# Two transformer blocks on one core: norm of the state-space branch two steps deep, rotary embedding moved to VectorE, and three edits of the order of weight splits and modulation products

## What is computed

```python
for l in range(2):      # first block: mod = silu(c) @ ada_w[l] + ada_b[l], nine vectors of 1024
    h = h + 0.5 * (1 + mod[2]) * swiglu(modulate(rmsnorm(h), mod[0], mod[1]), wg, wu, wd)
    proj = modulate(rmsnorm(h), mod[3], mod[4]) @ w_in
    y_ret = retention(rq, rk, rv, rg)       # rope(q), rope(k), decayed scores, rmsnorm, * silu(g)
    y_sb = stick_breaking(sq, sk, sv)
    y_ssm = mamba2(z, xbc, dt, ...)         # ends in rmsnorm(y * silu(z), norm_gain)
    h = h + (1 + mod[5]) * (concat(y_ret, y_sb, y_ssm) @ w_out)
    h = h + 0.5 * (1 + mod[8]) * swiglu(modulate(rmsnorm(h), mod[6], mod[7]), ...)

def rope(x):            # x1, x2: the lower and upper half of a head's 128 dimensions
    return concat([x1 * cos - x2 * sin, x1 * sin + x2 * cos])
```

## Time and profile before

| what | value |
|---|---|
| median of three runs | 1975.79 us (1975.63 to 1977.26) |
| the profiled execution | 1976.52 us, span 1974.4 us |
| TensorE busy | 1924.0 us (97%) |
| VectorE busy | 1499.2 us (76%) |
| ScalarE busy | 1065.5 us (54%) |
| GpSimd busy | 175.8 us (9%) |
| one split by ScalarE (L1334), by VectorE (L1914), one product (L1889) | mean 1045, 1234 and 1250 ns |
| granted TensorE clock | 0.997 of full speed, mean |

### The profile page before, as it was taken

One profiled execution on the slowest core, in us unless ns is written; L12 is line 12 of the kernel. 1 busy time (PEld: TensorE's weight loads), 2 busy tenths in 40 slices (PEclk: granted clock), 3 DMA queues, 4 the chain that ended last, 5 costly groups with the idle time before them and its releaser, 6 DMA issues.

```text
span 1974.4 us, 38148 instructions
## 1 busy us (share of the span) xinstructions
PE 1924.0 (97%) x15902; PEld 1881.0 (95%) x15902; DVE 1499.2 (76%) x2287; ACT 1065.5 (54%) x1712; POOL 175.8 (9%) x182
## 2 busy tenths in 40 slices
PE   7999999999999999999999999999999999999998
PEld 6999999899999999999899999999999999999998
DVE  7767787887787777878877787878777777788553
ACT  5644655474546544654664455465644455557453
POOL 0000012120011000022211000000210000002000
PEclk9999999999999999999999999999999999999999
DMA  9778575557785777666567865566587765555552
GB/s 379 281 258 320 185 261 203 203 207 259 268 318 212 264 276 262 217 226 224 208 248 281 300 224 197 192 206 234 199 284 275 269 223 195 200 208 189 194 193 107
DMA packets 83837, 466.40 MB, mean 236 GB/s; under 512 B 9424, under 2 KB 9552, under 8 KB 44496
## 3 DMA queue, kind: packets, MB, share of 16 engines
q1 hardware_dynamic: 48544, 334.98, 47.0%
q10 hardware_dynamic: 35120, 128.99, 18.4%
HBM read 462.88 MB, written 1.05 MB: 235 GB/s over the span
## 4 chain that ended last, share of the span: by engine, by line
PE 56%; DVE 9%; ACT 5%; issue 1%; POOL 0%; DVEq 0%; ACTq 0%
PE bank L737 55%; DVE low L1914 3%; ACT high L1334 2%; DVE ada_ring L1889 1%; PE bank L1135 1%; DVE u_split L1963 1%; DVE v L1956 0%; ACT full L1473 0%; DVE h L2060 0%; DVE region L2421 0%; ACT sil L1481 0%; DVE rope_t L2101 0%; ACT L1481 0%; DVE sil L2106 0%; ACT v L1355 0%
## 5 line engine op out<-in xcount | busy, mean ns | idle before, releaser
L1914 DVE TENSOR_TENSOR low<-ring,high 128x1024 fp32r<-128x1024 f32 x616 | 751.6, 1234 | 295.7 <-issue 179.5
L737 PE MATMUL bank<-u_split,high 128*128 128x256 f32 x5664 | 741.2, 280 | 9.2 <-DVE u_split L1963 5.1
L737 PEld LDWEIGHTS bank<-u_split,high 128*128 128x128 f32 x5664 | 691.9, 188 | 17.5 <-DVE u_split L1963 7.6
L1334 ACT ACTIVATE high<-ring 128x1024 fp32r<-128x1024 f32 x616 | 618.0, 1045 | 77.7 <-PE bank L737 51.2
L737 PE MATMUL bank<-u_split,low 128*128 128x256 f32 (+1 forms) x2832 | 410.2, 278 | 0.0
L737 PEld LDWEIGHTS bank<-u_split,low 128*128 128x128 f32 (+1 forms) x2832 | 362.9, 188 | 0.4
L1889 DVE SCALAR_TENSOR_TENSOR ada_ring<-ada_ring,cond 128x1024 f32<-128x1024 f32 x242 | 302.5, 1250 | 0.0
L737 PE MATMUL bank<-hid,high 128*128 128x256 f32 x2112 | 269.2, 277 | 0.0
L737 PEld LDWEIGHTS bank<-hid,high 128*128 128x128 f32 x2112 | 253.8, 188 | 0.0
L1533 ACT ACTIVATE sil<-bank 128x256 f32<-128x256 f32 x107 | 41.2, 385 | 199.5 <-PE bank L737 199.4
L737 PE MATMUL bank<-hid,low 128*128 128x256 f32 x1056 | 148.1, 277 | 0.0
(11 more groups left out here) (240 smaller groups left out, 2073.7 us busy)
## 6 DMA issues: line engine op xcount, KB each, us to landing
ring<-stream SPq DMA_DIRECT2D x302, 1024.0 KB, 5.8
ada_ring<-ada ACTq DMA_DIRECT2D x240, 512.0 KB, 4.5
region<-ada SPq DMA_DIRECT2D x6, 1024.0 KB, 12.9
ring<-stream SPq DMA_DIRECT2D x4, 640.0 KB, 4.8
region<-na_bias ACTq DMA_DIRECT2D x2, 1024.0 KB, 5.2
ring<-stream SPq DMA_DIRECT2D x4, 512.0 KB, 4.5
cst<-const SPq DMA_DIRECT2D x1, 1600.0 KB, 8.3
cond<-cond SPq DMA_DIRECT2D x2, 512.0 KB, 6.5
```

What stands on the lines that cost most here:

```text
L737: return pe.e.matmul(out, lhs, rhs, start=start, stop=stop, skip_group_check=True)
L1334: act.e.activation(hi, src, ACT.Copy).then_inc(*act.done(("high", n)))
L1914: dve.e.tensor_tensor(lo, src, hi.bitcast(F32), ALU.subtract).then_inc(*dve.done(("low", n)))
```

## The change

It has five parts.

1. Rotary embedding without TensorE and GpSimd: VectorE multiplies the bank by cos into SBUF, multiplies the two halves of the partitions by sin into a second tile, each half read from the other half's partitions and one with factor -1, and adds. This is done in the turn in which q and k are finished; the piece ret_rope, its matmul and its bank are gone.
2. The norm of the state-space branch scales tile j before it subtracts for tile j-1.
3. The four grains of the retention gate (sg) take no modulation products (rate 0 instead of 0.75).
4. wanted_first asks for one grain more in each of the turns 3 to 8, instead of one in each second turn.
5. In the down part of every feed-forward the additions (and ScalarE's squares) stand ahead of the turn's split and products.

```diff
-        side[18 + h].append((0, "ret_rope", h))
...
-    if key[0] in ("xbc", "dt", "sz"):
+    if key[0] in ("xbc", "dt", "sz", "sg"):
         return 0.0
-    if key[0] in ("sv", "sq", "sk", "sg", "rv", "rq", "rk"):
+    if key[0] in ("sv", "sq", "sk", "rv", "rq", "rk"):
         return RATE_HEADS
...
-    return 18 if t < 3 else 19 if t < 5 else 20 if t < 7 else 21
+    return 18 + max(0, t - 2)
...
         for n in range(FT):
-            split(first + 2 * FT + n + 1 + AHEAD)
-            ada(dve.ada.turns(rate_of(("down", f, n))))
             for d in range(KT - 1):
                 if SUMMED[d] == n - 1:
                     add(d)
+            split(first + 2 * FT + n + 1 + AHEAD)
+            ada(dve.ada.turns(rate_of(("down", f, n))))
         add(KT - 1)
...
-                    for j in range(4):
-                        y = m.sy[:, j, :]
-                        dve.e.scalar_tensor_tensor(out=y, in0=y, scalar=m.pa(l, "sgn", j, 1), in1=r, op0=ALU.mult,
-                                                   op1=ALU.mult).then_inc(*dve.done(("ssm_scaled", l, j)))
-                        dve.wait_ge(("y_high", l, 8 + j))
-                        rest(m.y_sb, 4 + j, y, ("y", l, 8 + j))
+                    for j in range(5):
+                        if j < 4:
+                            y = m.sy[:, j, :]
+                            dve.e.scalar_tensor_tensor(out=y, in0=y, scalar=m.pa(l, "sgn", j, 1), in1=r, op0=ALU.mult,
+                                                       op1=ALU.mult).then_inc(*dve.done(("ssm_scaled", l, j)))
+                        if j:
+                            dve.wait_ge(("y_high", l, 7 + j))
+                            rest(m.y_sb, 3 + j, m.sy[:, j - 1, :], ("y", l, 7 + j))
...
             dve.wait_ge(("full", "rqk", l, h))
-            copy(m.rqk[:, h, :], m.banks[dve.bank("rqk", l, h)], ("out", "rqk", l, h), ("rqk", l, h))
+            dve.e.tensor_tensor(two(m.rqk[:, h, :]), two(b), spread(cos, 2), ALU.mult).then_inc(*dve.done(("ret_cos", l, h)))
+            if h:
+                dve.wait_ge(("roped", l, h - 1))
+            dve.e.scalar_tensor_tensor(out=two(t2[up]), in0=two(b[down]), scalar=-1.0, in1=spread(sin[down], 2), op0=ALU.mult,
+                                       op1=ALU.mult).then_inc(*dve.done(("ret_sin", l, h)))
+            dve.e.tensor_tensor(two(t2[down]), two(b[up]), spread(sin[up], 2), ALU.mult) \
+                .then_inc(*dve.done(("out", "rqk", l, h), ("ret_sin", l, h)))
+            dve.wait_ge(("ret_cos", l, h), ("ret_sin", l, h))
+            dve.e.tensor_tensor(m.rqk[:, h, :], m.rqk[:, h, :], t2, ALU.add).then_inc(*dve.done(("roped", l, h)))
```

More of the change, by code:

```diff
@@ L1056, in side @@
                     values(b, m.sv, i, m.tb[3 * (i % 2) + 1]).then_inc(*pe.done(("sb_values", l, i)))
-                elif piece == "ret_rope":
-                    b = banks.take("work", "ret_rope", l, i)
-                    pe.wait_ge(("rqk", l, i))
-                    mm(b[:, 0:2 * T], m.c1("rot"), m.rqk[:, i, :], True, True).then_inc(*pe.done(("ret_rot", l, i)))
                 elif piece == "ret_scores":
@@ L2261, in side @@
                     rest(m.y_sb, i, b[:, 0:T], ("out", "sb_values", l, i), ("y", l, 4 + i))
-                elif piece == "ret_rope":
-                    b = m.banks[dve.bank("ret_rope", l, i)]
-                    t1, t2 = m.rope_t[:, 0:512], m.rope_t[:, 512:1024]
-                    dve.wait_ge(("ret_rot", l, i))
-                    if i:
-                        dve.wait_ge(("roped", l, i - 1))
-                    dve.e.tensor_tensor(two(t2), two(b[:, 0:512]), spread(m.c1("sin"), 2), ALU.mult) \
-                        .then_inc(*dve.done(("out", "ret_rope", l, i), ("ret_sin", l, i)))
-                    dve.wait_ge(("ret_cos", l, i), ("ret_sin", l, i))
-                    dve.e.tensor_tensor(m.rqk[:, i, :], t1, t2, ALU.add).then_inc(*dve.done(("roped", l, i)))
                 elif piece == "ret_scores":
@@ L2577, in side @@
                     pool.e.tensor_tensor(w, w, m.c1("before"), ALU.mult).then_inc(*pool.done(("sb_weight", l, i)))
-                elif piece == "ret_rope":
-                    pool.wait_ge(("rqk", l, i))
-                    if i:
-                        pool.wait_ge(("roped", l, i - 1))
-                    pool.e.tensor_tensor(two(m.rope_t[:, 0:512]), two(m.rqk[:, i, :]), spread(m.c1("cos"), 2), ALU.mult) \
-                        .then_inc(*pool.done(("ret_cos", l, i)))
                 elif piece == "ret_norm":
```

4 lines of the change are left out of this document (3 added, 1 removed).

## The result

The changed kernel takes 1984.56 us (median of 4 runs, 1984.06 to 1986.92), the kernel before 1975.71 beside it: ratio 1.0047, 95% interval 1.003 to 1.0063. It is slower by more than the 0.2% that can be told. That is 8.8 us more by the medians. The forecast was 1979.1, 3.3 us more, with a range of 1971.5 to 1985.5.

A forecast was written before the change was run, and what follows sets the result against it. TensorE, fed during 1924.0 of 1974.4 us, was taken as the bound. Terms -6.6 (rope, norm), +8.0 and +2.2 (sg products), 0.0 (splits), -0.3 (additions) summed to +3.3: 1979.1 us, range 1971.5 to 1985.5.

The forecast's parts named there:

- Rope and norm, -6.6: Both layers' mixers: parts 1 and 2 together save 3.3 us a layer, between 1.5 and 5.
- a new wait eats most of the two rotations, and 0.5 is left: Ahead of the state-space norm: TensorE gains 1.6 us, then waits 1.1 for ScalarE's last square.
- The retention wait: TensorE's wait for the first retention head's square, 1.20 us before; TensorE was to go on 1.6 us earlier.
- the slow product of 2.04 at 344.09: First mixer: a modulation product slowed from 1.21 us beside GpSimd's product; removing that gives back 0.8 to 1.1 a head.
- The burst, +8.0: Second feed-forward, behind the third addition: five products instead of one, with stands for loads, cost 8.0 us (4.6 to 10).
- Ahead of the second block, +2.2: Two missing products of 1.14 us delay the gain columns and TensorE's first matmul there by 2.2 us (1.8 to 2.5).
- First feed-forward, 0.0: Part 4: the 1.54 us wait at 79.68 goes but returns as about 1.5 near 86.3; between -1.6 and +0.6.
- Additions first, -0.3: Part 5: stages end with a less late last addition; -0.3 us over four feed-forwards, between -1 and +1.
- (b): First feed-forward: without the wait, TensorE's quick pace saves 4.6 us plus 1.5 of wait, giving 1973.0; chance 0.1.
- Rival (a): Second feed-forward: loads land in time, the five products cost 2 us instead of 8, giving 1973.1; chance 0.15.
- (d): Second feed-forward's five products cost little and the rope pays in full: 10 us below forecast, 1969; chance 0.05.
- Rival (c): Mixers: VectorE's extra rope work holds TensorE longer, a layer keeps 1 us, -2 instead of -6.6, 1983.7; chance 0.2.

The follow-up runs named there:

- sg undone: The changed kernel with the retention gate's four grains taking modulation products again (0.75 each); 1977.19 us, ratio 0.9999.
- the other pair: Kernel before with deeper norm, earlier splits and additions ahead of splits (ratio 0.998), against the same without the additions moved (1970.85 us, 0.9972).
- two experiments: Changed kernel with rate 0.46 in the second feed-forward's gate and up part, 1.0031; kernel before with deeper norm and products moved out of its down part, 0.9991.
- additions first alone: The kernel before with only the additions and squares put ahead of the splits and products in the down parts; ratio 1.0005.
- rope behind side: Changed kernel with the retention gate's products restored and VectorE's four rope instructions per head behind the turn's mixer pieces; 1973.91 us, ratio 0.9994.
- later products: Kernel before, deeper norm, rate 0.45 in the second feed-forward's down part, 0.46 in gate and up parts of second and third; 1974.46 us, ratio 0.9991.
- the first four: First experiments: changed kernel with part 3 undone (1977.19 us); kernel before with part 3 (1990.01), part 1 (1978.05) or part 2 (1972.58) only.

## Why the prediction came out as it did

The sign and the place of the loss were right, the size was not: 3.3 forecast, 8.8 measured, near the upper end of the range. By its own steps, with the slow excess taken out:

**Rope and norm, -6.6.** Measured -2.6 and -3.2, in sum -5.8. The sum was nearly right by luck, for its make-up was wrong. I gave the matmuls that go most of it, and the norm the rest; alone, the rope is worth -1.1 and the norm about -4 (-5.3 in its one trace, with the clock drop that before has and it has not). The step that failed is "a new wait eats most of the two rotations, and 0.5 is left" together with what followed it: nothing was left. The rotations' own price was right: at the ones matmuls TensorE was 2.90 us ahead (354.51 against 357.41), 1.17 of it from the start of the stage, so 0.87 for each of the two where I had 0.8. The new wait was 1.43 against 1.1. The retention wait, which I had shrinking below 1.2, grew to 1.88, since TensorE comes earlier and VectorE, against the start of the stage, does not: ScalarE's square was at 367.61 and is at 366.52, 1.09 earlier in a stage that began 1.17 earlier. The norm's part I gave 1.7 us of tiles, and the four tiles took 5.2 us before and 3.3 in the change (1.9 less); but I counted it within a chain that the rope had already lengthened. Alone it removed the wait of 1.20 altogether.

One input was misread. I charged the slow product of 2.04 at 344.09 to the rope's work on GpSimd. It takes 2.04 in the changed kernel too, beside another GpSimd product of 1.03 that was there before (rows above). The two further places in the kernel before did give back 1.1 each, as this pair shows (the other is two splits at 357.77 that took 3.43 instead of 2.35):

```profile
348.41 2.13 POOL L2582 TENSOR_TENSOR rope_t<-region,cst 128x512 f32<-128x512 f32 x1 [1.13 <-DVE region L2271]
...
349.31 2.31 DVE L1889 SCALAR_TENSOR_TENSOR ada_ring<-ada_ring,cond 128x1024 f32<-128x1024 f32 x1
```

So ahead of the last square VectorE got 1.1 back where I had 1.8, and a head cost 2.84 where I had 2.5. By my own sum that is 2 x 2.84 - 2.6 - 1.1 = 2.0 late, not 0.6. The square came 1.0 later in a stage that began 1.17 earlier: 2.2. This is the term that was mis-sized most.

**The burst, +8.0.** Measured 7.9 (changed kernel against sg undone), 7.5 alone. The stands for loads were 4.16, within the 2 to 5. But it did not come about as I had it. I had VectorE's loss come out at the end of the stage, and the wait there was 1.24, as before (1.26). TensorE lost 6.08 at one grain, for ScalarE, which stood behind the load issues, and 1.4 behind it to the clock. I had 1.5 for ScalarE and no term for the clock, so that the 8.0 came out is in part luck. The stage as a whole grew by 9.4; the other 1.5 belongs to the additions.

**Ahead of the second block, +2.2.** Measured 2.35 by the wait (0.55 to 2.90), and 1.3 more for the lower clock behind it, for which the forecast had nothing. By the stage it is 2.7 against sg undone and 4.0 against before, which scatter by 1.3.

**First feed-forward, 0.0.** Measured -0.9, -1.25 as it ran. The wait came back at 86.97, where I had 86.3, and was 0.87 where I had 1.5. Kernels with the old order differ by 2.5 in this stage, so 0.0 can't be told from what was measured.

**Additions first, -0.3.** Failed in sign: +1.6 in the second feed-forward, +2.4 in the other pair. I argued from TensorE's reads, which set the time in the other stages; in this one VectorE does, as I had written two paragraphs earlier. With the addition first its gain columns also need the product that the same turn would have taken, so a second one stands ahead of the split.

**The rest.** -5.8 + 7.9 + 2.7 - 0.9 + 1.6 is 5.5; the span grew by 7.8, of which 1.5 is slow excess, and 0.8 I cannot place in this scatter. Against the forecast of 3.3, most of the difference is in the additions (1.9), the second block (0.5 to 1.8), the slow excess (1.5) and the mixers (0.8). The rival that TensorE keeps its quick pace in the first feed-forward (b) is refuted as priced: three kernels ran the stage fast from its start, and the quick pace saved 4.5 us of matmuls for 2.0 to 2.8 more of wait at its end than before had. Rival (a) is refuted by the 6.08, and (d) with it. Rival (c), which had each layer keep 1 us, fits the rope alone (1.0 and 0.1) and not the two parts together.

## What to carry to other kernels

Before you move work from an engine that is always fed to one that waits, look at what stands behind the move on the second engine: removing its round trips (the norm) was worth about 4 us, giving it work in exchange for matmuls was worth nothing. Work that is done "on the way" must be counted at its deadlines: three products were free when spread over 44 grains and cost 9 us at the next vector that needed them. Look there at every engine that issues something for the work: the grain that TensorE missed was held by load issues in ScalarE's program. And a long wait of TensorE costs more than its length, by the lower clock behind it. A rate with fractions moves all that follow; two experiments fixed one stage and lost about 5 us elsewhere in that way.

## What the runs showed of the hardware

**Two paces at full clock.** In every trace 256-column matmuls come every 113 or every 118 ns in long stretches, with a granted clock of 1.00 in both. The pace changes at interruptions of the stream (a wait, a float32 piece, two small matmuls) and can last a whole feed-forward. Which one a stretch gets differs between executions of equal code: the first feed-forward was slow from about 80 us on in most of the traces, and fast throughout in those of additions first, rope behind side and later products. Between 90 and 200 us the changed kernel did 937 matmuls, the one with additions first alone 972:

```profile
90.00:200.00 110.00, 110.00 (x972) 109.96 (x971) 82.28 (x115) 50.47 (x68) 3.70 (x5) 1.00 0.81 285
```

The slow excess is 16 to 27 us in the 14 profiled executions. That is a spread of 11 us, as wide as that of one kernel's times (1972.5 to 1983.9 for the kernel before, beside the first four), but that the one makes the other is not shown. What decides the pace is open.

**The lower clock behind waits.** After waits of TensorE of 2.90, 4.94 and 6.08 us the granted clock was 0.50 to 0.58 for some us of matmuls (rows above). After a wait of 2.20 us it was 0.59 in one execution and 1.00 in another whose code is the same up to there.

**A VectorE instruction on 64 partitions costs what one on 128 does:** 0.69 us for 64x512 and for 128x512 out of a bank (rows above).

**GpSimd and VectorE hold each other up, by the kind of operand.** The product with two tensors in SBUF took 2.31 us beside GpSimd's cos product, 1.22 else; the sin product, which reads a bank, took 0.68 beside another cos product (345.01 to 347.28) in the kernel before:

```profile
346.79 0.68 DVE L2268 TENSOR_TENSOR rope_t<-bank,cst 128x512 f32<-128x512 f32 x1
```

The Trainium skill says that the two engines contend when a VectorE instruction has two SBUF inputs (GPSIMD Engine Reference, Specifications); both rows agree with it.

More can be read from the trace of the kernel before. A split, which also has two SBUF inputs, was not slowed by the cos product that began 0.23 us behind it, and another cos product, which began while VectorE stood idle, took 1.29:

```profile
348.18 1.22 DVE L1914 TENSOR_TENSOR low<-ring,high 128x1024 fp32r<-128x1024 f32 x1
...
374.61 1.29 POOL L2582 TENSOR_TENSOR rope_t<-region,cst 128x512 f32<-128x512 f32 x1
```

The split ended at 349.40, the cos product that took 2.13 us at 350.54, VectorE's product that took 2.31 us at 351.62: each about 1.1 behind the one before. So here the two engines took turns by whole instructions, and the one that came second stood.
